# Recurrent stage: preparation reordered over three engines, blocks transposed out of the banks, pair products in two pairs of banks

## The reference, cut to what matters

```python
w = -softplus(-(w0 + tanh(wd) @ w2)) - 0.5
decay = exp(-exp(w))
a = sigmoid(a0 + ad @ a2)
g = sigmoid(gd) @ g2
kk = k * k_k;  kk = kk * rsqrt(max(sum(kk * kk, head), 1e-24))
k = k * (1 + (a - 1) * k_a)
def step(state, r, w, k, v, kk, a):          # one token, one head
    sa = state @ (-kk)
    state = state * w + outer(sa, kk * a) + outer(v, k)
    return state, state @ r
y = groupnorm(scan(step)) + sum(r * k * r_k, head) * v
```

## Time and profile before

| what | us |
|---|---|
| median of three runs | 1454.34 (1453.39 to 1454.66) |
| the profiled execution's own time | 1456.48 |
| its span | 1454.7 |
| the stage's preparation up to the gathered blocks (284.66 to 344.03) | 59.4 |
| the substitution (344.03 to 384.94) | 40.9 |
| the chunks (384.94 to 475.67) | 90.7 |
| TensorE busy over the span | 1326.3 |
| VectorE | 1028.0 |
| ScalarE | 612.7 |
| GpSimd | 254.3 |

### The profile page before, as it was taken

One profiled execution on the slowest core, in us unless ns is written; L12 is line 12 of the kernel. 1 busy time (PEld: TensorE's weight loads), 2 busy tenths in 40 slices (PEclk: granted clock), 3 DMA queues, 4 the chain that ended last, 5 costly groups with the idle time before them and its releaser, 6 DMA issues. The chain is left out here.

```text
span 1454.7 us, 18771 instructions
## 1 busy us (share of the span) xinstructions
PE 1326.3 (91%) x5765; PEld 919.6 (63%) x5765; DVE 1028.0 (71%) x1669; ACT 612.7 (42%) x927; POOL 254.3 (17%) x329
## 2 busy tenths in 40 slices
PE   5989999966799999995999999999999999999938
...
GB/s 328 198 214 231 74 158 145 73 0 1 1 1 59 297 106 96 98 76 202 322 348 357 346 359 351 355 347 354 385 382 353 347 348 346 356 346 304 122 231 354
DMA packets 86737, 340.80 MB, mean 234 GB/s; under 512 B 16982, under 2 KB 22296, under 8 KB 59556
## 3 DMA queue, kind: packets, MB, share of 16 engines
...
## 5 line engine op out<-in xcount | busy, mean ns | idle before, releaser
L2225 DVE TENSOR_TENSOR gate_up_low<-gate_up,gate_up_high 128x1024 fp32r<-128x1024 f32 x204 | 244.8, 1221 | 42.5 <-ACT gate_up_high L2116 39.0
L2197 PE MATMUL py<-down_ring,hT 128*128 128x512 f32 x544 | 250.0, 602 | 0.9 <-ACT hT L2135 0.9
L2158 PE MATMUL p_gate_up<-gate_up_high,x_hi 128*128 128x512 f32 x544 | 242.2, 445 | 5.3 <-DVE x_lo L2234 5.3
L2158 PE MATMUL p_gate_up<-gate_up_low,x_hi 128*128 128x512 f32 x544 | 216.8, 399 | 0.0
L2158 PE MATMUL p_gate_up<-gate_up_high,x_lo 128*128 128x512 f32 x544 | 215.8, 397 | 0.0
L2116 ACT ACTIVATE gate_up_high<-gate_up 128x1024 fp32r<-128x1024 f32 x204 | 203.6, 1051 | 0.7 <-PEq L1381 0.7
L2197 PEld LDWEIGHTS py<-down_ring,hT 128*128 128x128 f32 x544 | 98.0, 190 | 98.8 <-issue 98.7
L2158 PEld LDWEIGHTS p_gate_up<-gate_up_high,x_hi 128*128 128x128 f32 x544 | 104.0, 191 | 45.2 <-issue 21.5
L2158 PEld LDWEIGHTS p_gate_up<-gate_up_high,x_lo 128*128 128x128 f32 x544 | 103.7, 191 | 29.7 <-issue 10.6
L2087 POOL TENSOR_TENSOR carrier<-offsets 1x1 f32<-1x1 f32 x136 | 28.4, 209 | 521.9 <-DVE tokens L2243 474.4
L460 PE MATMUL pz<-h_hi,w_hi 128*128 128x512 f32 x288 | 116.9, 406 | 1.7 <-DVE ring_lo L537 1.7
...
## 6 DMA issues: line engine op xcount, KB each, us to landing
...
```

What stands on the lines that cost most here:

```text
L2158: mm = pe.matmul(pgu[u % 2][:, :], x[:, u % 2, k, :], weights, start=(k == 0 and n == 0), stop=(k == KD - 1 and n == 2))
L2197: mm = pe.matmul(py[half][:, :], hT[:, u % 2, k, :], weights[:, k, half * N:half * N + N], start=(k == 0), stop=(k == 1))
L2225: V.tensor_tensor(moe.low[u % RING][:, :, piece(i), :], moe.gate_up[u % RING][:, :, piece(i), :], exact(w_hi[:, u % 2, :, piece(i), :]), A ...
```

## The change

Nothing of what is computed changes. What does:

- TensorE makes the LoRA products for decay and `a` together (banks 0 to 3 and 4 to 7), then the sums of squares, then the gate's.
- ScalarE takes `mid`, `last`, `bonus` and the convolution's mean from VectorE, squares kk between the sigmoids, and makes the exponentials grouped by kind: `sg`, then the growing one into a buffer of its own (`grown`, in `XS`), and `ep` last.
- VectorE's order is scans, centring, the factor of k, the maxima, the subtraction, k times factor, the r_k product, A times root, b times A. It multiplies b by the growing exponential (from GpSimd) and gives r times `ep` to GpSimd. `bonus` times v has both inputs in SBUF now.
- GpSimd clears `XS` after k and r, since `XS` holds `grown` and `root` (the inverse norm) until then.
- VectorE transposes the 32-blocks straight out of the banks. ScalarE alone copies the banks, eight copies, after the transposes.
- Pair products alternate between banks 0, 1 and banks 6, 7 for the first three chunks, and kind 0 of the next chunk is made after `y_of_v`.

```diff
+        grown, root = early(XS, 0), early(XS, 1)
...
+        def pair_bank(n):
+            return 6 if n % 2 and n < KINDS * LAST_C else 0
...
-            pool.wait_ge(s_rk, RT_)
-            for r in range(RT_):
-                pool.wait_ge(s_e2, r + 1)
-                pool.tensor_tensor(aB[:, r, :], aB[:, r, :], cum[:, r, :], ALU.mult).then_inc(s_bop, 1)
-            for r in range(RT_):
-                pool.tensor_tensor(k_[:, r, :], k_[:, r, :], cum[:, r, :], ALU.mult).then_inc(s_kop, 1)
+            pool.wait_ge(s_bop, RT_)
+            for r in range(RT_):
+                pool.tensor_tensor(k_[:, r, :], k_[:, r, :], grown[:, r, :], ALU.mult).then_inc(s_kop, 1)
+            pool.wait_ge(s_e1, RT_)
+            for r in range(RT_):
+                pool.tensor_tensor(r_[:, r, :], r_[:, r, :], ep[:, r, :], ALU.mult).then_inc(s_rop, 1)
+            pool.wait_ge(s_kop, RT_)
+            pool.memset(XS[:, :, :, :], 0.0).then_inc(s_clear, 1)
...
+            kk_squared(0)
+            kk_squared(1)
+            for r in range(RT_):
+                act.wait_ge(s_lora, r + 1)
+                act.activation(sg[:, r, :], bank(r), ACT.Sigmoid, bias=vcol("w0", r)).then_inc(s_loraA, 1)
+                if r < 2:
+                    kk_squared(r + 2)
+                if r:
+                    middle(r - 1)
+            middle(RT_ - 1)
...
+            for r in range(RT_):
+                act.wait_ge(s_lora, 2 * RT_ + r + 1)
+                act.activation(gate_r[:, r, :], bank(4 + r), ACT.Copy).then_inc(s_loraA, 1)
+            act.wait_ge(s_half, RT_)
+            act.activation(mid_e[:, :, :], mid[:, :, :], ACT.Exp, scale=-DECAY).then_inc(s_mid, 1)
             for r in range(RT_):
                 act.wait_ge(s_cc, r + 1)
-                if r == 0:
-                    act.activation(mid_e[:, :, :], mid[:, :, :], ACT.Exp, scale=-DECAY).then_inc(s_mid, 1)
                 act.activation(sg[:, r, :], sg[:, r, :], ACT.Exp, scale=-DECAY).then_inc(s_e3, 1)
+            for r in range(RT_):
+                act.activation(grown[:, r, :], cum[:, r, :], ACT.Exp, scale=DECAY).then_inc(s_e2, 1)
+            for r in range(RT_):
+                act.wait_ge(s_rksum, r + 1)
+                act.activation(bonus[:, r, :], bank(r), ACT.Copy).then_inc(s_rkA, 1)
+            act.wait_ge(s_cm, 1)
+            act.activation(conv_stat, bank(4), ACT.Copy, scale=1.0 / CW).then_inc(s_cmV, 1)
+            act.wait_ge(s_kF, RT_)
+            for r in range(RT_):
+                act.activation(last[:, r, :], cum[:, r, P - 1::P], ACT.Exp, scale=-DECAY).then_inc(s_last, 1)
                 act.activation(ep[:, r, :], cum[:, r, :], ACT.Exp, scale=-DECAY).then_inc(s_e1, 1)
-                act.wait_ge(s_e1, r + 1)
-                act.activation(cum[:, r, :], cum[:, r, :], ACT.Exp, scale=DECAY).then_inc(s_e2, 1)
-
-            act.wait_ge(s_kop, RT_)
+
             act.wait_ge(s_aop, RT_)
-            act.wait_ge(s_rop, RT_)
+            act.wait_ge(s_e1, RT_)
+            act.wait_ge(s_last, RT_)
+            act.wait_ge(s_L32, P // B)
             for c in range(NT):
                 act.wait_ge(s_T, c + 1)
-                act.activation(ABT[:, c, 0:RT_, :], tiles(2 * c), ACT.Copy).then_inc(s_TA, 1)
+                for q in range(2):
+                    act.activation(ABT[:, c, RT_ * q:RT_ * q + RT_, :], tiles(2 * c + q), ACT.Copy).then_inc(s_TA, 1)
...
-                    if j:
-                        pe.wait_ge(s_loraA, RT_ * (j - 1) + r + 1)
-                    pe.matmul(bank(r), weights[:, r * P:(r + 1) * P], inputs, start=True, stop=True).then_inc(s_lora, 1)
-                if j == 0:
-                    pe.wait_ge(s_io, 10)
+                    if j == 2:
+                        pe.wait_ge(s_loraA, RT_ + r + 1)
+                    pe.matmul(bank(r if j == 0 else 4 + r), weights[:, r * P:(r + 1) * P], inputs, start=True, stop=True).then_inc(s_lora, 1)
...
                     for r in range(RT_):
+                        pe.wait_ge(s_loraA, r + 1)
                         pe.wait_ge(s_kksq, r + 1)
-                        pe.matmul(bank(4 + r), headones[:, :], bonus[:, r, :], start=True, stop=True).then_inc(s_kksum, 1)
-            pe.wait_ge(s_kkmax, RT_)
-            for r in range(RT_):
+                        pe.matmul(bank(r), headones[:, :], bonus[:, r, :], start=True, stop=True).then_inc(s_kksum, 1)
+            for r in range(RT_):
+                pe.wait_ge(s_kkmax, r + 1)
                 pe.wait_ge(s_rk, r + 1)
-                pe.matmul(bank(4 + r), headones[:, :], bonus[:, r, :], start=True, stop=True).then_inc(s_rksum, 1)
+                pe.matmul(bank(r), headones[:, :], bonus[:, r, :], start=True, stop=True).then_inc(s_rksum, 1)
...
-                if n:
+                if n >= KINDS * LAST_C:
                     pe.wait_ge(s_pairV, n)
+                elif n >= 2:
+                    pe.wait_ge(s_pairV, n - 1)
                 for r in range(RT_):
                     for q in range(2):
-                        mm = operand((r, q), lhs, rhs, c, tiles(q)[:, r, :])
+                        mm = operand((r, q), lhs, rhs, c, tiles(pair_bank(n) + q)[:, r, :])
                 mm.then_inc(s_pair, 1)
...
-            pe.wait_ge(s_TA, NT)
-            pe.wait_ge(s_TV, NT)
+            pe.wait_ge(s_TA, 2)
             pe.wait_ge(s_kop, RT_)
-            pe.wait_ge(s_rop, RT_)
+            pairs(0, 0)
+            pe.wait_ge(s_TA, 4)
             for c in range(LAST_C):
                 turn_k(c)
                 turn_v(c)
-                pairs(c, 0)
+                if c == 0:
+                    pe.wait_ge(s_rop, RT_)
+                    pe.wait_ge(s_TA, 2 * NT)
                 pairs(c, 1)
                 g_of_v(c)
                 pairs(c, 2)
                 y_of_v(c)
+                if c + 1 < LAST_C:
+                    pairs(c + 1, 0)
                 kv(c)
                 turn_b(c)
...
             for r in range(RT_):
                 dve.wait_ge(s_kkroot, r + 1)
-                done[r] = link.sign(V.tensor_tensor(A[:, r, :], A[:, r, :], bonus[:, r, :], ALU.mult))
+                done[r] = link.sign(V.tensor_tensor(A[:, r, :], A[:, r, :], root[:, r, :], ALU.mult))
             for r in range(RT_):
                 link.wait(done[r])
                 done[r] = link.sign(V.tensor_tensor(aB[:, r, :], aB[:, r, :], A[:, r, :], ALU.mult))
             for r in range(RT_):
+                dve.wait_ge(s_e3, r + 1)
                 link.wait(done[r])
-                V.scalar_tensor_tensor(out=bonus[:, r, :], in0=k_[:, r, :], scalar=vcol("r_k", r), in1=r_[:, r, :],
-                                       op0=ALU.mult, op1=ALU.mult).then_inc(s_rk, 1)
-            link.wait()
-
-            for r in range(RT_):
-                dve.wait_ge(s_e3, r + 1)
                 V.scalar_tensor_tensor(out=A[:, r, :], in0=A[:, r, :], scalar=-1.0, in1=sg[:, r, :], op0=ALU.mult,
                                        op1=ALU.mult).then_inc(s_aop, 1)
-                dve.wait_ge(s_rksum, r + 1)
-                V.tensor_tensor(bonus[:, r, :], bank(4 + r), v_[:, r, :], ALU.mult).then_inc(s_bonus, 1)
-            dve.wait_ge(s_cm, 1)
-            V.tensor_scalar(conv_stat, bank(0), 1.0 / CW, None, ALU.mult).then_inc(s_cmV, 1)
-            dve.wait_ge(s_rk, RT_)
-            for r in range(RT_):
-                dve.wait_ge(s_e1, r + 1)
-                link.sign(V.tensor_copy(last[:, r, :], ep[:, r, P - 1::P]))
-                V.tensor_tensor(r_[:, r, :], r_[:, r, :], ep[:, r, :], ALU.mult).then_inc(s_rop, 1)
-            link.wait()
+                dve.wait_ge(s_e2, r + 1)
+                V.tensor_tensor(aB[:, r, :], aB[:, r, :], grown[:, r, :], ALU.mult).then_inc(s_bop, 1)
+            for r in range(RT_):
+                dve.wait_ge(s_rkA, r + 1)
+                V.tensor_tensor(bonus[:, r, :], bonus[:, r, :], v_[:, r, :], ALU.mult).then_inc(s_bonus, 1)
             dve.wait_ge(s_mid, 1)
+            dve.wait_ge(s_last, RT_)
             V.tensor_tensor(hop[:, :, 0:NT - 1], last[:, :, 0:NT - 1], mid_e[:, :, 1:NT], ALU.mult).then_inc(s_hop, 1)
-            dve.wait_ge(s_kop, RT_)
-            dve.wait_ge(s_aop, RT_)
-            for c in range(NT):
-                dve.wait_ge(s_T, c + 1)
-                V.tensor_copy(ABT[:, c, RT_:HEADS, :], tiles(2 * c + 1)).then_inc(s_TV, 1)
-            dve.wait_ge(s_TV, NT)
-            dve.wait_ge(s_TA, NT)
-            every = ABT[:, :, :, :].rearrange("p c h t -> p (c h) t")
+            dve.wait_ge(s_T, NT)
+            every = psum[:, :].rearrange("p (g t) -> p g t", t=P)
             for b in range(P // B):
                 rows = slice(B * b, B * b + B)
-                V.transpose(L32[rows, :, :], every[rows, :, rows].rearrange("p c t -> p t c")).then_inc(s_L32, 1)
+                V.transpose(L32[rows, :, :], every[rows, :, rows].rearrange("p g t -> p t g")).then_inc(s_L32, 1)
```

96 lines of the change are left out of this document (51 added, 45 removed).

## The result

| | before | after |
|---|---|---|
| median of the runs, us | 1454.5 (4 runs, 1453.39 to 1456.92) | 1434.8 (4 runs, 1433.78 to 1439.23) |
| ratio to before, 95% interval | | 0.9865 (0.984 to 0.9891) |
| the profiled execution, its span | 1456.48, 1454.7 | 1433.78, 1431.9 |

The change gains 19.7 us; the forecast was 8.4 us, and 1434.8 lies under its range (1440 to 1452). The profiled executions differ by 22.7 us, of which 2 lie ahead of the stage, in work that the change doesn't touch: VectorE's first instruction of the stage starts at 284.70 in before and at 282.67 in after. In the later runs it starts anywhere from 279.4 to 286.4, and 13 executions of before on one chip took 1448.04 to 1460.26 us. So I compare the stage's parts, counted from that first instruction ("of the stage"), and use whole times to confirm.

A forecast was written before the change was run, and what follows sets the result against it. VectorE was taken to bound preparation and solve (the latter with waits for TensorE), TensorE the tail. Gains of 6.2 us up to the gathering and 2.2 in the solve made 8.4: 1445.9 us against the median, range 1440 to 1452.

The forecast's parts named there:

- Part 1: Preparation up to the T products, priced to the last b operand: about 3.4 us gained.
- rival 2: Covers in the preparation hold better than thought: 1443.4 or 1441.8 us, with both cases 1439.3; chance 0.19.
- rival 2's first case: TensorE's clock is high from the first sums of squares: 2.5 us more gained, time 1443.4 us.
- Part 2: From the T products to the gathered 32-row blocks: about 2.8 us gained.
- rival 2's second case: `bonus` times v takes no turns with GpSimd: 3.1 us, and 1 at `hop`, time 1441.8 us.
- The lower bound (half): For the four transposes out of the banks, priced at 7.73 us: at best half of 7.7 us less.
- Part 3: The solve of the 32-row blocks: about 2.2 us gained, VectorE waiting 4.9 to 5.0 us for TensorE instead of 7.2.
- nobody waits for it: GpSimd's queue behind k (r, memset of `X`) ends with the gathering and delays nobody; no cost priced.
- Turn-taking at the transposes (1): Each transpose out of a bank waits for one GpSimd r multiplication: 4.4 us lost, 1450.3 us; chance 0.10.
- Rival 3: In the solve the second pair of banks brings nothing: the 2.2 us fall away, 1448.1 us; within the 0.56.
- Rival 4: Transposes out of the banks are slower: from 4.0 us each the change loses, at 5.0 each 1458.2 us; chance 0.06.
- a band of 5 us: Whole kernel: time between 1443.5 and 1448.5 us, with the case of no gain from the second banks in it; chance 0.56.

The follow-up runs named there:

- e11: Kernel after, with the LoRA products for a waiting until the four for the decay have ended; 1441.35 us, ratio 0.9898.
- e6: Kernel after, with each `bonus` times v product waiting for the one before it to end; 1433.18 us, ratio 0.9844.
- e7: Kernel after, with GpSimd's r split by chunks and its later parts and the b scalings released beside masks; 1427.39 us, ratio 0.9811.
- e3: Kernel after, with pair products in banks 0 and 1 alone and in the order of before; 1437.22 us, ratio 0.9904.
- e10: Kernel after, with one pair of banks and no pair product made ahead except the very first, ahead of the turns; 1438.38 us, ratio 0.9886.
- e1: Kernel before, with transposes straight out of banks, ScalarE making all eight copies after them, first pair product ahead of the turns; 1445.76 us, ratio 0.9956.

## Why the prediction was wrong

The sign, the bounding engines and the untouched tail were right. Five steps failed.

- **Part 1, "Four more of the same kind end at 292.3 + 6.8 = 299.1"**: wrong. The LoRA products for a run beside those for the decay. Worth 3.6 us (e11 against e6). This is the largest miss, and no bound of mine covered it: I had given products one behind the other no second value.
- **Part 1, "So I let the squares' sums start at 299.1 with three at 1.70"**: the clock rose at 8.8 us of the stage, ahead of the sums, and four took 3.70 us and not 5.9. At the last b operand that is 1.5 us more (after against e6). That is rival 2's first case, which I had at 2.5. The rest of part 1 was right: VectorE has no gap from the last maximum on, and e11, which restores the assumed order, lands on 38.5 of 38.6 us.
- **Part 2, "the next three take turns with GpSimd at 1.68 each"**: wrong, 3.2 us (11.8 against 8.6, e6). The operations at 1038 ns alternate with L1221, which reads a bank; there GpSimd gets in. I read each 1.68 us there as one instruction of either engine, but it held two of VectorE's, L1218 at 1.15 and L1221 at 0.68. Four in a row leave GpSimd no opening: rival 2's second case, priced at 3.1.
- **Part 2, "A whole-bank copy out of PSUM takes 676 ns and a product out of SBUF 684 ..., so the source should not matter"**: mis-sized, 7.73 us against 5.07, 2.7 us. Those rows compare contiguous reads; the transposes read every 128th number. The lower bound (half) had the possibility in it. What the Trainium skill, PSUM — Partial Sum Buffer, Specifications, says of matmuls would, carried over to VectorE, have made the transposes slower than out of SBUF; they were faster, and the measurement decides. The Trainium skill, Vector Engine (DVE) Microarchitecture Reference, Measured stream behaviour on trn2, has for SBUF that a program with one input hopping 4 KiB on every element takes 1.73 ns a column and not 1.054. The trace agrees in kind, for another instruction with hops of 512 bytes: 1.93 us / 1024 = 1.88 ns out of SBUF. Out of a bank it is 1.24 / 1024 = 1.21.
- **Part 3, "the second pair of banks does not help there"**: the sum was near (3.4 us against 2.2) and the account wrong on both sides. I held the whole first chunk at the lower clock as in before. With the new order and the second pair of banks the rise came at 7.8 us and not 14.5, and all 7.2 us of waits at masks went. GpSimd, which now reaches into the substitution, took 4.0 us back: e7, which keeps it out, needs 33.5 us. I had written of its queue "nobody waits for it": nobody waits for its result, but VectorE waits for its turn.

Together 3.6 + 1.5 + 3.2 + 2.7 + 1.2 = 12.2 us beyond the 8.4, which makes 20.6 of the stage's 20.7.

The rivals. Turn-taking at the transposes (1) did not occur: they took 1245 ns in the median while GpSimd multiplied, so with the rule of the Trainium skill, SBUF — State Buffer, Who interferes with whom, the trace agrees. The waits came behind them, in the substitution. Rival 2 occurred in both halves, at 0.19 chance. Rival 3 is refuted by e3 and e10 (6.9 and 5.6 us longer in the substitution), with GpSimd where the change puts it; e1 gained 3.2 us there with one pair of banks. Rival 4, slow transposes, is refuted by the trace. My error in the chances was one of kind: I listed good surprises for the clock and the turns only, and put 0.56 on a band of 5 us in which each of four prices had to hold.
